# One 8 KB row per pick instead of two 4 KB rows, and 192 gathered tokens in the second layer

## The reference

```python
q = (h @ w_q).reshape(t, 8, 2, 128)
s = jnp.einsum('thpd,hpnd->thpn', q, sub_keys)          # 128 scores per head and side
sv, si = lax.top_k(s, 16)
cand = sv[:, :, 0, :, None] + sv[:, :, 1, None, :]
best, ci = lax.top_k(cand.reshape(t, 8, 256), 16)       # 16 picks per head
experts = i1 * 128 + i2                                 # (t, 128), of 16384 experts
gates = jax.nn.softmax(best, axis=-1)                   # (t, 128)
a = jnp.einsum('td,tkd->tk', h, u_tab[experts])
w = gates * jax.nn.gelu(a, approximate=False)
y = jnp.einsum('tk,tkd->td', w, v_tab[experts])         # x = x + mod[5] * y
```

## Time and profile before

| | |
|---|---|
| median of 3 runs | 5421.61 us (5421.06 to 5422.04) |
| profiled execution, its own time | 5423.36 us |
| its span | 5421.5 us |
| mean granted TensorE clock | 0.878 |
| PE, DVE, ACT, POOL busy | 85%, 69%, 30%, 26% of the span |
| moved by DMA | 899 MB, 166 GB/s in the mean |

### The profile page before, as it was taken

One profiled execution on the slowest core, in us unless ns is written; L12 is line 12 of the kernel. 1 busy time (PEld: TensorE's weight loads), 2 busy tenths in 40 slices (PEclk: granted clock), 3 DMA queues, 4 the chain that ended last, 5 costly groups with the idle time before them and its releaser, 6 DMA issues. The chain is left out here.

```text
span 5421.5 us, 73867 instructions
## 1 busy us (share of the span) xinstructions
PE 4614.3 (85%) x24885; PEld 3965.5 (73%) x24885; DVE 3735.4 (69%) x7428; ACT 1635.4 (30%) x2249; POOL 1409.0 (26%) x1600
## 2 busy tenths in 40 slices
PE   5976588869878999999999976657782799999998
PEld 4966355658876888888888765624561699999998
DVE  1147433338998888889999933823379878888887
ACT  1221233321033332232322332234320333333332
POOL 0000000000077444444444400000001933333332
PEclk9975577789589999999999988568895999999999
DMA  3110011111345999999999910000110477877786
GB/s 118 62 36 1 15 39 36 46 55 51 118 165 213 314 314 315 313 312 314 315 314 312 308 52 20 1 15 1 38 60 22 180 275 278 278 275 275 272 275 229
DMA packets 232172, 898.98 MB, mean 166 GB/s; under 512 B 26160, under 2 KB 26192, under 8 KB 226656
## 3 DMA queue, kind: packets, MB, share of 16 engines
q0 software_dynamic: 129440, 474.96, 25.7%
q1 hardware_dynamic: 102528, 421.57, 22.1%
HBM read 835.61 MB, written 60.82 MB: 165 GB/s over the span
## 5 line engine op out<-in xcount | busy, mean ns | idle before, releaser
L419 PE MATMUL psA<-h_hi,split_hi 128*128 128x512 f32 (+2 forms) x2816 | 1018.1, 362 | 109.2 <-DVE h_lo L1495 64.6
L419 PE MATMUL psA<-h_lo,split_hi 128*128 128x512 f32 (+2 forms) x2816 | 1014.2, 360 | 0.0
L419 PE MATMUL psA<-h_hi,split_lo 128*128 128x512 f32 (+2 forms) x2816 | 1013.7, 360 | 0.0
L1477 DVE TENSOR_TENSOR split_lo<-raw,split_hi 128x1024 fp32r<-128x1024 f32 x596 | 727.4, 1220 | 227.7 <-ACT split_hi L1084 217.6
L419 PEld LDWEIGHTS psA<-h_hi,split_hi 128*128 128x128 f32 x2816 | 533.4, 189 | 172.8 <-DVE h_lo L1495 66.3
L1084 ACT ACTIVATE split_hi<-raw 128x1024 fp32r<-128x1024 f32 x596 | 629.8, 1057 | 90.8 <-PE psV L419 76.3
L1404 ACT ACTIVATE W_hi<-gel 128x512 fp32r<-128x512 f32 (+1 forms) x256 | 148.4, 580 | 1495.4 <-DVE gel L1952 1495.4
L419 PEld LDWEIGHTS psA<-h_hi,split_lo 128*128 128x128 f32 x2816 | 533.1, 189 | 60.3
L419 PEld LDWEIGHTS psA<-h_lo,split_hi 128*128 128x128 f32 x2816 | 533.5, 189 | 59.1
L1050 POOL DMA_INDIRECT rows<-pv,pick_i x384 | 459.0, 1195 | 404.9 <-DVE y_tok L1990 344.7
L1962 DVE SCALAR_TENSOR_TENSOR xT<-psA,mod,xT 128x512 f32<-128x512 f32 (+1 forms) x512 | 349.8, 683 | 308.0 <-PE psA L419 305.7
(11 more groups left out here) (278 smaller groups left out, 7639.2 us busy)
## 6 DMA issues: line engine op xcount, KB each, us to landing
raw<-tiles SPq DMA_DIRECT2D x596, 512.0 KB, 5.3
gates<-g_buf SPq DMA_DIRECT2D x28, 2048.0 KB, 6.4
raw<-mod_tiles SPq DMA_DIRECT2D x80, 512.0 KB, 3.2
g_in<-gates POOLq DMA_DIRECT2D x64, 512.0 KB, 9.3
g_in<-gates POOLq DMA_DIRECT2D x64, 384.0 KB, 5.9
mod_w<-mod_pairs SPq DMA_DIRECT2D x8, 1024.0 KB, 18.3
rows<-pu,pick_i POOLq DMA_INDIRECT x384, 7.4
rows<-pv,pick_i POOLq DMA_INDIRECT x384, 7.3
```

The costliest lines, as they stand in the source:

```text
L419: ins = nc.tensor.matmul(out_, lhsT, rhs, start=start, stop=stop)
L1477: V.tensor_tensor(split_lo[:, n % SPLIT].rearrange("p k n -> p (k n)"), raw[:, n % RAW, :], split_hi[:, n % SPLIT].rearrange("p k n -> p ( ...
```

## The change

- The two tables are joined on the host into one of 16384 rows of 8 KB, u and v side by side (`rows0`, `rows1`). A unit is now one pick for u and v together: one gather of 128 rows of 8 KB, a dot product on the first half, gelu and gate on ACT (`weigh`, two one-column activations), and the sum with the second half. The ring has 4 buffers of 8 KB in layer one and 6 in layer two (`RINGS`).
- In layer two 192 tokens are gathered and 320 are dense. The last 64 of the 192 are laid out as two halves of 64 partitions with 64 picks each, so layer two has 192 units, 3 per round. A 128 by 64 matrix `ident2` adds the halves when `y_tok` is transposed back. `build_gates` has 10 blocks there instead of 12.
- With 320 columns, six chunks of v and the pieces of two more fit into PSUM: in layer two all are resident, nothing is cycled. The two split chunks are made of pieces of 192 and 128 columns.
- Expert tiles are loaded in pairs of 1 MB, 8 KB for each partition.
- PE now makes the last transposes after the resident chunks have been added (`residents_added`).

```diff
-RING = 7
+RINGS = (4, 6)
-DENSE = ((NCTX, NLAT), (NCTX, NLAT - P))
-GATHERED = ((0, 1), (NTT - 1,))
+HALF = P // 2
+DENSE = ((NCTX, NLAT), (NCTX + P + HALF, NLAT - P - HALF))
+GATHERED = (((0, P), (P, P)), ((NCTX, P), (NCTX + P, HALF)))
 PICKS = PH * TOPK
-PASSES = tuple(tuple((part, j) for part in range(2) for j in range(len(g))) for g in GATHERED)
-UNITS = tuple(len(p) * PICKS for p in PASSES)
+UNITS = tuple(sum(PICKS * n // P for _, n in g) for g in GATHERED)
-RESIDENT, CYCLED = (1, 3, 5, 7), (0, 2, 4, 6)
+RESIDENT = (tuple((2 * q + 1, 0, NLAT, q, 0) for q in range(4)),
+            tuple((k, 0, DENSE[1][1], k, 0) for k in range(6)) +
+            ((6, 0, 192, 0, 320), (6, 192, 320, 1, 320), (7, 0, 192, 2, 320), (7, 192, 320, 3, 320)))
+CYCLED = ((0, 2, 4, 6), ())
...
+        def load_pair(n, where):
+
+            sp.wait_ge(hi_done, seen.at(hi_done, n + 2 - RAW))
+            sp.wait_ge(lo_done, seen.at(lo_done, n + 2 - RAW))
+            sp.dma_start(raw[:, n % RAW:n % RAW + 2, :], expert_pairs[where]).then_inc(raw_landed[n % RAW], 16)
...
             def gather(u):
 
-                part, j, e = pick(l, u)
-                b = (UNIT0[l] + u) % RING
-                if UNIT0[l] + u >= RING:
-                    pool.wait_ge(row_used, UNIT0[l] + u - RING + 1)
-                nc.gpsimd.indirect_dma_start(rows[:, b, :], None, ((pu0, pv0), (pu1, pv1))[l][part],
-                                             bass.IndirectOffsetOnAxis(pick_i[:, j, e:e + 1], 0))\
+                b = u % RINGS[l]
+                if u >= RINGS[l]:
+                    pool.wait_ge(row_used, UNIT0[l] + u - RINGS[l] + 1)
+                if u == PICKS and GATHERED[l][1][1] == HALF:
+                    pool.wait_ge(pick_moved, 32)
+                nc.gpsimd.indirect_dma_start(rows[l][:, b, :], None, (rows0, rows1)[l],
+                                             bass.IndirectOffsetOnAxis(pick_i[:, u:u + 1], 0))\
                     .then_inc(rows_landed[b], 16)
...
+            def weigh(count):
+
+                for _ in range(count):
+                    u = unit[0]
+                    unit[0] += 1
+                    if u == PICKS and GATHERED[l][1][1] == HALF:
+                        act.wait_ge(pick_moved, 32)
+                    w = pick_w[:, u:u + 1]
+                    act.wait_ge(dot_done, UNIT0[l] + u + 1)
+                    A(w, w, ACT.Gelu).then_inc(act_chain, 1)
+                    act.wait_ge(act_chain, seen.upto(act_chain))
+                    A(w, w, ACT.Copy, scale=pick_g[:, u:u + 1]).then_inc(pick_gated, 1)
...
+            def dot(u):
+
+                j, _ = pick(l, u)
+                b = u % RINGS[l]
+                h_ = h_tok[:, :, j * P:(j + 1) * P]
+                row = rows[l][:, b, 0:D].rearrange("p (k t) -> p k t", t=P)
+                dve.wait_ge(rows_landed[b], seen.upto(rows_landed[b], 16))
+                V.tensor_tensor_reduce(row, row, h_, 1.0, 0.0, ALU.mult, ALU.add, pick_w[:, u:u + 1]).then_inc(dot_done, 1)
+
+            def accumulate(u):
+
+                j, first = pick(l, u)
+                row = rows[l][:, u % RINGS[l], D:2 * D].rearrange("p (k t) -> p k t", t=P)
+                y_ = y_tok[:, :, j * P:(j + 1) * P]
+                dve.wait_ge(pick_gated, UNIT0[l] + u + 1)
...
+            pe.wait_ge(y_ready, seen.upto(y_ready))
+            pe.wait_ge(residents_added, seen.upto(residents_added))
```

More of the change, by code:

```diff
@@ L85, in route_order @@
 def route_order(layer):
-    s, n = DENSE[layer]
-    return list(GATHERED[layer]) + list(range(s // P, (s + n) // P))
+    whole = [s // P for s, n in GATHERED[layer] if n == P]
+    return whole + list(range(DENSE[layer][0] // P, NTT))
 def segs_of(layer, context_too):
@@ L916, in load @@
                 sp.wait_ge(lo_done, seen.at(lo_done, n - RAW + 1))
-            sp.dma_start(raw[:, n % RAW, :], tiles[n if where is None else where])\
+            sp.dma_start(raw[:, n % RAW, :], tiles[tile_row(n) if where is None else where])\
                .then_inc(raw_landed[n % RAW], 16)
@@ new lines, in accumulate @@
+            def accumulate(u):
[3 more added lines that the diff above has]
+                dve.wait_ge(pick_gated, UNIT0[l] + u + 1)
+                if first:
+                    ins = V.tensor_scalar(y_, row, pick_w[:, u:u + 1], None, ALU.mult)
+                else:
+                    dve.wait_ge(row_used, UNIT0[l] + u)
+                    ins = V.scalar_tensor_tensor(y_, row, pick_w[:, u:u + 1], y_, ALU.mult, ALU.add)
+                ins.then_inc(row_used, 1)
@@ L1972, in rows_used, with row_work @@
+            def row_work(count):
                 for _ in range(count):
-                    u = unit[0]
+                    k = unit[0]
                     unit[0] += 1
-                    part, j, e = pick(l, u)
-                    b = (UNIT0[l] + u) % RING
-                    row = rows[:, b, :].rearrange("p (k t) -> p k t", t=P)
-                    h_, y_ = h_tok[:, :, j * P:(j + 1) * P], y_tok[:, :, j * P:(j + 1) * P]
-                    if part == 1 and e == 0:
-                        dve.wait_ge(pick_gelu, seen.upto(pick_gelu))
-                        V.tensor_tensor(pick_w[:, j], pick_w[:, j], pick_g[:, j], ALU.mult).then_inc(dve_chain, 1)
-                        dve.wait_ge(dve_chain, seen.upto(dve_chain))
@@ L1991, in rows_used @@
-                    ins.then_inc(row_used, 1)
-            extra = share == 8
+                    if k == 0:
+                        dot(0)
+                    elif k % 2 and (k + 1) // 2 < UNITS[l]:
+                        dot((k + 1) // 2)
+                    elif k < 2 * UNITS[l]:
+                        accumulate(k // 2 - 1 if k % 2 == 0 else UNITS[l] - 1)
+            four = share == 4
             dve.wait_ge(htok_ready, seen.upto(htok_ready))
```

266 lines of the change are left out of this document (156 added, 110 removed).

## The result

| | before | after |
|---|---|---|
| time, median (us) | 5421.34 (5419.58 to 5422.04, 4 runs) | 5324.27 (5323.81 to 5325.83, 4 runs) |
| profiled execution: time, span (us) | 5423.36, 5421.5 | 5323.81, 5322.0 |
| mean granted clock of TensorE | 0.878 | 0.876 |

The ratio of the times, after to before, is 0.9822, with a 95% interval of 0.9805 to 0.9839: 97 us faster, and 0.3 us from the forecast. The change itself, timed again beside later kernels, gave 5324.98 us (0.9808 to 0.9835 of before).

A forecast was written before the change was run, and what follows sets the result against it. PE was taken to set the pace; after the change PE, the DVE-ACT loop and DMA all want about 15.0 us. Terms -85.8 - 22.7 + 10.5 = -98.0 us gave 5324 us, 8-in-10 range 5297 to 5395 us.

The forecast's parts named there:

- PE: 14.99 us: Layer two, PE's round: 84 matmuls of 320 columns, 12.31 us, plus 24 narrow ones at 0.1116 us, 2.68 us.
- Rival five: Layer two: narrow matmul pieces cost as much as 384 columns, round 16.5 us, time 5399 us; chance 0.03.
- The loop of DVE and ACT: Layer two: dot products, ACT pairs, splits and sums form a loop of 14.56 us, 14.97 with four handovers.
- Rival two: Layer two: ACT chain longer, 1.0 us for a pair instead of 0.5, round 15.97 us, 5367 us; chance 0.13.
- The 0.3 us for waits that add up: Layer two: 0.3 us added to three things wanting about 15.0, round 15.3 us, -85.8 us over 64 rounds.
- DMA: Layer two: 5.57 MB a round, 13.2 us at 421 GB/s or 16.1 at 340 to 345; taken as 15.0.
- rival one: Layer two: DMA engines become the bound at 345 GB/s, round 16.15 us, time 5378 us; chance 0.19.
- four: Layer two: DMA engines move no more than 313 GB/s, round 17.8 us, slower at 5484 us; chance 0.07.
- Gate blocks: Building gates in layer two: two fewer blocks, 16 fewer of 96 copies, -22.7 us.
- Layer one at 0: Layer one: same matmuls, dot products and sums, a 1.36 us DVE wait covering handovers; costed at 0.
- rival three: Layer one: 1 MB landing over 15 us or handovers beyond 1.36 us, +32 us, 5356 us; chance 0.08.
- Ends: Layer two's tail +4.5 us, layer one's +1.0, starts of both +4, route +1: together +10.5 us.

The follow-up runs named there:

- experiment 1: Changed kernel with each pick's gelu and gate moved behind ACT's high split of their place, layer two only: 5301.32 us.
- experiment 3: Changed kernel with layer two gathering only the u half of each row, 4 KB a pick, and summing that half: 5308.67 us.
- experiment 4: Changed kernel without the 128-column matmuls in all but the first and last round of layer two: 5328.48 us.
- 2: Changed kernel without ACT's gelu and gate of each gathered pick in layer two: 5300.63 us.
- 7: Changed kernel with ACT's gelu and gate moved behind the high split and only 4 KB u rows gathered, both in layer two: 5296.66 us.
- 5: Changed kernel with layer two back to 128 gathered and 384 dense tokens and cycled chunks, 8 KB rows and paired loads kept: 5434.81 us.
- experiment 6: Changed kernel with expert tiles loaded singly, 512 KB each, in both layers: 5319.05 us.

## Why the prediction was right, point by point

- **PE's pace and the pieces.** The step "PE: 14.99 us" rested on 192 and 128 columns both sitting on a floor of 0.11 us. The trace shows just that, and where TensorE is never idle (experiment 1) 108 matmuls take 750 / 5398 x 108 = 15.01 us. Rival five is excluded. By the Trainium skill, "TensorE: Matmul & The Clock Gate", section "Wait — 56ns, not 53.3ns?", the round would have been about 13.1 us on PE, an estimate from its spacing; the trace's 15.01 us disagrees with that for these operands, as the earlier trace rows had said it would.
- **The loop of DVE and ACT.** "14.97 us" with "four handovers at 0.1 each". The undisturbed round is 15.17 (experiment 3). A pair took 0.43 us, not 0.5, and its rows are 0.20 and 0.29 us. DVE's waits for ACT came as named, each under 0.6 us in the round shown. The loop's sum has two of them, which come to 0.44 and 0.57 us with its handovers (0.24 and 0.37 over DVE's own 13.95, and 0.1 for each handover); they measured 0.36 and 0.48. It has nothing for the third, 0.29 us, before the last low split: ACT's high part waits 3.09 us for DVE's product, and both splits of the v tiles, with a pair between them, stand behind it. ACT's own waits for dot products were 0.67 and 2.72 us, not under 0.6, and the second is the one that holds the split back. The mechanism was right and it was the bound: less TensorE work gave nothing (experiment 4), while taking the pair away, or moving it, gave 23 us (1 and 2), and with half rows moving it still gave 9.8 us of the stage (3 and 7). I had written that it "hides under PE by nothing at all", and then left it at three things wanting 15.0. It was the one that ended last. Rival two (1.0 us for a pair) is excluded.
- **The 0.3 us for waits that add up.** This was judgement, on top of 15.0, and it was 0.41: rounds averaging 15.41 us between low parts of c = 1 (4320.6 to 5291.6, 63 rounds). Of that 0.24 is due to rows and DMA (experiment 3), and 0.17 is the loop's own. The stage gave 80.8 us, 5.0 less than the 85.8 I took.
- **DMA.** I took 15.0 us from the 4 us window in the earlier trace rows; the rounds moved 362 GB/s, and 371 after the reorder, both above the 345 of rival one. Rivals one and four are excluded. DVE waited for rows 0.25 us a round (13.1 us in 800) and PE for low splits 0.22 (11.7), under the 0.5 that I named as the first sign of being wrong. The figure of about 358 GB/s that the prediction took from the Trainium skill is, by its page "DMA: Bandwidth & Descriptors", section "Measured (HBM→SBUF, 128 partitions, SWDGE, issued from GpSimd)", what each core gets when both cores of a pair stream, and a core alone has 425 GB/s there in a transfer of 16 MB. One core runs here, and 371 to 372 GB/s over 750 us agree with that reading; no run here has a neighbour streaming.
- **Gate blocks.** -22.7 forecast, -23.1 measured.
- **Layer one at 0.** Its low parts start from 1731.9 to 3113.0 us, before from 1731.9 to 3112.9; rival three is excluded. A landing of 7.5 us for 1 MB is far from the 15 us allowed.
- **Ends.** This was mis-sized: +10.5 forecast, 1.3 - 2.5 + 5.5 = +4.3 measured. The step "Starts ... taken as +4 for both" is the one that failed: layer two starts 2.5 us sooner, since the first gates land sooner and the first dot product had its rows in time. Layer two's tail was +4.5 by forecast and +5.5 measured, and that agreement is in part luck. The additions and transposes themselves take 11.0 us, not 8.75 (4.26 before), since DVE waits 2.08 and 1.15 us for transposes where the sum had 0.9 once; but they begin 1.2 us sooner after the last low part, which the sum had at nothing.

The forecast of 5324 against 5324.27 is thus better than its terms: the rounds saved 5 us less and the ends cost 6 us less. Each term was right to some 6 us, and that is the accuracy to credit it with; the 0.3 us is luck.

What stays open: what it would give to issue the gathers ahead of POOL's wait for the gates (experiments 1 and 5), which the rows suggest and no run tried, and whether a DMA share of 0.96 would leave room for it; whether the token split would give the whole gain with 4 KB rows; and whether single loads help the change by the 5 us between the medians.

## What to carry to other kernels

When a small step of one engine (here 0.43 us on ACT) waits for a late producer, cost what stands behind it in its queue, not its own time: put work that is ready ahead of the wait. Look for the same pattern in every queue: POOL's gathers stand behind a wait of 8 to 11 us in each round of layer two. When several resources come out within 0.2 us of each other, add up something for their collisions, and don't expect relief of one to show: only the two together moved the time here (3 and 5 us alone, 75 together). And of a change with several parts, time the part that you believe in by its absence; the rows in one pass and the paired loads, without the token split, made this kernel 0.2% slower.

## What the runs showed that I had not expected

- Gathers of 8 KB pieces mixed with weight loads and gate loads sustain 371 to 372 GB/s for 750 us at a share of 0.96, with a median landing of 10.1 to 10.3 us for 1 MB. The same core's layer one shows 312 at 0.85.
- The GB/s at a given share depends on the pieces: 313 at 0.92 before, 312 at 0.85 after, for the same bytes in layer one. With the weights loaded singly (experiment 6) and the 8 KB rows kept it is 312 at 0.91, so most of the difference comes from the weight loads.
- A one-column activation takes 0.20 us (gelu) or 0.29 us (copy with a scale read from SBUF), and the pair 0.43 us from start to start of the next instruction.
- The dot product's result comes from a separate accumulator read of 0.08 us; the next DVE instruction starts at the same time (both at 4665.57 us in the round shown), so that it costs nothing on DVE.
